# Odd attention: turning the weights on two 64-row halves, with their copies shared anew and four half chunks cast by GpSimd's transfers

## The reference, cut to what matters

```python
H_C, H_C_KV, DH_C = 16, 2, 64       # 16 query heads, 2 key/value heads
s = q @ k.T * 64 ** -0.5 + bias      # banded: own chunk of 64 and the two before
s = where(valid, s, NEG_INF)
p = softmax(concat([s, sink]))[..., :-1]
o = p @ v                            # (S, 16 * 64)
y = o @ w_out                        # 1024 x 1024
```

## Time and profile before

| | |
|---|---|
| median of 3 runs | 1346.29 us (1346.19 to 1346.6) |
| profiled execution | 1346.09 us |
| its span | 1344.2 us |
| TensorE matmuls busy | 1334.3 us, 99% |
| DVE, ACT, GpSimd busy | 974.3, 740.2, 125.3 us |
| granted TensorE clock | 0.999 of full |
| odd attention | about 1079 to 1111 us from the span's start |

### The profile page before, as it was taken

One profiled execution on the slowest core, in us unless ns is written; L12 is line 12 of the kernel. 1 busy time (PEld: TensorE's weight loads), 2 busy tenths in 40 slices (PEclk: granted clock), 3 DMA queues, 4 the chain that ended last, 5 costly groups with the idle time before them and its releaser, 6 DMA issues.

```text
span 1344.2 us, 19217 instructions
## 1 busy us (share of the span) xinstructions
PE 1334.3 (99%) x7365; PEld 1121.7 (83%) x7365; DVE 974.3 (72%) x1502; ACT 740.2 (55%) x1155; POOL 125.3 (9%) x114
## 2 busy tenths in 40 slices
PE   9999999999999999999999999999999999999998
PEld 6888888888888888888888777888888878888886
DVE  7566878777664767877778687886667887786665
ACT  6564555554545754555445676754445675654443
POOL 1000011111000000311111002220000010400000
PEclk9999999999999999999999999999999999999999
DMA  9743545555455334656655524357765524355552
GB/s 375 246 153 129 187 158 193 187 195 192 173 219 186 127 126 160 228 200 231 202 189 201 170 95 151 117 216 227 216 204 193 182 79 173 119 206 193 191 191 88
DMA packets 37673, 244.32 MB, mean 182 GB/s; under 512 B 4656, under 2 KB 5312, under 8 KB 10192
## 3 DMA queue, kind: packets, MB, share of 16 engines
q1 hardware_dynamic: 33568, 228.08, 47.9%
q0 software_dynamic: 3728, 14.82, 3.9%
q10 hardware_dynamic: 288, 0.21, 0.1%
HBM read 241.13 MB, written 1.97 MB: 181 GB/s over the span
## 4 chain that ended last, share of the span: by engine, by line
PE 97%; DVE 1%; ACT 1%; DMA 0%; issue 0%; POOL 0%; ACTq 0%; DVEq 0%
PE ps L1217 19%; PE ps L1155 17%; PE ps L1161 16%; PE ps L1164 16%; PE ps L1224 10%; PE ps L1323 3%; PE ps L1418 2%; PE ps L1449 2%; PE ps L1400 1%; PE ps L2034 1%; PE ps L1265 1%; PE ps L1259 1%; PE ps L1262 1%; PE ps L1577 1%; PE ps L2044 1%; PE ps L1578 1%
## 5 line engine op out<-in xcount | busy, mean ns | idle before, releaser
L2736 DVE TENSOR_TENSOR wlo<-raw,whi 128x1024 fp32r<-128x1024 f32 (+2 forms) x423 | 510.4, 1217 | 264.2 <-ACT whi L2151 263.1
L2151 ACT CAST whi<-raw 128x1024 fp32r<-128x1024 f32 (+1 forms) x431 | 444.6, 1041 | 332.9 <-PE ps L1224 188.5
L1217 PE MATMUL ps<-act,whi 128*128 128x512 f32 x1120 | 266.4, 390 | 0.0
L1217 PEld LDWEIGHTS ps<-act,whi 128*128 128x128 f32 x1120 | 208.4, 188 | 42.2
L1155 PE MATMUL ps<-whi,mhi 128*128 128x512 f32 (+2 forms) x688 | 235.7, 392 | 0.3 <-DVE mlo L2760 0.3
L1161 PE MATMUL ps<-wlo,mhi 128*128 128x512 f32 (+2 forms) x688 | 231.1, 385 | 0.0
L1164 PE MATMUL ps<-whi,mlo 128*128 128x512 f32 (+2 forms) x688 | 231.0, 385 | 0.0
L1164 PEld LDWEIGHTS ps<-whi,mlo 128*128 128x128 f32 x688 | 129.2, 188 | 26.4
L1161 PEld LDWEIGHTS ps<-wlo,mhi 128*128 128x128 f32 x688 | 129.2, 188 | 26.1 <-DVE wlo L2736 0.5
L1224 PEld LDWEIGHTS ps<-act,wlo 128*128 128x128 f32 x1120 | 143.6, 191 | 5.5
L1155 PEld LDWEIGHTS ps<-whi,mhi 128*128 128x128 f32 x688 | 125.9, 188 | 24.1 <-issue 2.4
(11 more groups left out here) (334 smaller groups left out, 1516.3 us busy)
## 6 DMA issues: line engine op xcount, KB each, us to landing
raw<-in_weights SPq DMA_DIRECT2D x210, 1024.0 KB, 4.8
gain_b<-in_norm_g POOLq DMA_DIRECT2D x6, 512.0 KB, 4.0
raw<-in_weights SPq DMA_DIRECT2D x5, 512.0 KB, 5.8
region<-in_b_gate POOLq DMA_DIRECT2D x2, 1024.0 KB, 8.6
o_nat<-in_mem_turned POOLq DMA_DIRECT2D x2, 1024.0 KB, 7.2
region<-band POOLq DMA_DIRECT2D x8, 256.0 KB, 5.0
region<-band POOLq DMA_DIRECT2D x8, 192.0 KB, 5.9
x<-in_x SPq DMA_DIRECT2D x1, 1024.0 KB, 11.6
```

What stands on the lines that cost most here:

```text
L1217: nc.tensor.matmul(ps[:, bank0 + f, :], of(whi, h)[:, k, f * P:f * P + P], act2[:, kx].rearrange("p i n -> p (i n)"), start=kx == 0, stop= ...
L2151: nc.scalar.copy(whi[:, m % HL, 0:w], raw[:, n % RAW, h * w:h * w + w]).then_inc(hi_done, 1)
L2736: nc.vector.tensor_tensor(wlo[:, m % HL, 0:w], raw[:, n % RAW, h * w:h * w + w], whi[:, m % HL, 0:w].bitcast(F32), ALU.subtract).then_inc( ...
```

## The change

`turn` for the odd attention now turns each 128 x 128 block by two transposes of 64 rows, with the identity's matching 64 x 64 part. The halves f = 0 and 1 go to banks 4 and 5. A group takes 384 columns of both banks. `at_x` rises by four behind the group's last transpose, in place of one for each unit. Before a group's first unit TensorE also waits for the copy of the second pair of the group before. The copies read both banks in strips of 64 columns and write the same layout as before. Groups 0, 8, 16 and 24 are now copied by DVE (both pairs), groups 4, 12, 20 and 28 by ACT (both pairs, between its second and third exponential).

The high parts of the four half chunks of `od_w_out`'s first job (0 to 3) are no longer cast by ACT. GpSimd issues a transfer for each, from the weights in HBM straight to the fp32r place in `whi`, as soon as TensorE is done with the half chunk four before it. The issues stand before its first `spread_weights`. ACT skips them; whoever waited for ACT's count waits for the transfer's own semaphore, and DVE's low part waits for the raw chunk too. Every other `wait_ge(hi_done, ...)` becomes `wait_hi`, with the count less the skipped ones.

```diff
--- before.py
+++ after.py
@@ -616,8 +618,10 @@
                     eng = "act" if d["joint"] or d["qt"] else "dve"
+                elif d["deep"]:
+                    eng = ("dve", "dve", "dve", "act")[i // 2 % 4]
                 else:
-                    eng = (("dve", "dve", "dve", "act") if d["deep"] else ("act", "dve", "dve", "dve"))[i // 2 % 4]
+                    eng = ("dve", "act")[i // 4 % 2]
                 n_copies[eng] += d["wide"] or i % (4 if d["joint"] else 2) == 0
@@ -625,6 +629,15 @@
                              [2 * plan.jobs["wo", l][0] + 1 for l in range(DEPTH)] + [2 * plan.jobs["w1", l, 0][0] for l in range(DEPTH)])
+
+        hi_by_dma = [2 * plan.jobs["out2", 1, 0][0] + h for h in range(4)]
+
+        def wait_hi(eng, m):
+
+            if m in hi_by_dma:
+                eng.wait_ge(hi_loaded[hi_by_dma.index(m)], 16)
+            else:
+                eng.wait_ge(hi_done, m + 1 - sum(k < m for k in hi_by_dma))
 
@@ -777,6 +790,16 @@
 
+        def turned_at(u, d):
+
+            return P * (u // 2 % 2), d["w"] // 2
+
+        def turned_by_rows(u, d, b, f):
+
+            first, w = turned_at(u, d)
+            at = first + w * (u % 2) + HD * b
+            return ps[:, 4 + f, at:at + HD]
+
         def pair_width(d):
@@ -785,6 +808,9 @@
                 return ps[:, 4 + d["pair"] % 2, 0:pair_width(d)]
+            if d["halved"]:
+                first, w = turned_at(u, d)
+                return ps[:, 4:6, first:first + 2 * w].rearrange("p f (b j) -> p f b j", j=HD)
             return ps[:, 4 + u // 2 % 2, 0:pair_width(d)]
@@ -798,6 +824,8 @@
                 at = 3072 + 768 * (d["pair"] % 2) + SEQ * d["qt"]
+            if pair and d["halved"]:
+                return work[:, at:at + pair_width(d)].rearrange("p (b f j) -> p f b j", f=2, j=HD)
             if pair:
@@ -1067,6 +1095,12 @@
                                               rden[:, :, HG * g:HG * g + HG].unsqueeze(3).to_broadcast([P, TT, HG, HD])).then_inc(shares_spread, 1)
+
+                    for i, m in enumerate(hi_by_dma):
+
+                        pool.wait_ge(pe_out, 2 * (m - HL + 1))
+                        weights, h = plan.chunks[m // 2][2], m % 2
+                        pool.dma_start(whi[:, m % HL, :], weights[:, h * HALF:h * HALF + HALF]).then_inc(hi_loaded[i], 16)
 
@@ -1413,6 +1447,17 @@
                         wait_copied(pe, u - back)
+                    if d["halved"]:
+
+                        if i % 4 == 0:
+                            wait_copied(pe, u - 2)
+                        for b in range(d["w"] // P):
+                            for f in range(2):
+                                rows_ = slice(HD * f, HD * f + HD)
+                                mm = nc.tensor.transpose(turned_by_rows(u, d, b, f), step_of(1536, u, d)[rows_, b * P:b * P + P], ident[rows_, rows_])
+                        if i % 4 == 3:
+                            mm.then_inc(at_x, 4)
+                        return
                     for b in range(d["w"] // P):
@@ -2133,6 +2178,9 @@
                     m = n_split[0]
+                    if m in hi_by_dma:
+                        n_split[0] += 1
+                        continue
                     n, h = divmod(m, 2)
@@ -2219,12 +2267,12 @@
                             exponents(i + 1)
-                        j = i - 4
-                        if j >= 0 and copied_by[u0 + j][0] == "act":
-                            act.wait_ge(at_x, u0 + j + 2)
-
-                            act.wait_ge(at_o, u0 + j - 4)
-                            nc.scalar.copy(values_of(u0 + j, us[j], True), turned_pair(u0 + j, us[j])).then_inc(at_ya, 1)
+                        for j in (i - 4, i - 2):
+                            if j >= 0 and copied_by[u0 + j][0] == "act":
+                                act.wait_ge(at_x, u0 + j + 2)
+
+                                act.wait_ge(at_o, u0 + j - 4)
+                                nc.scalar.copy(values_of(u0 + j, us[j], True), turned_pair(u0 + j, us[j])).then_inc(at_ya, 1)
                         each(i, True)
@@ -2728,7 +2776,9 @@
                     w = kc // 2 * cols
-                    dve.wait_ge(hi_done, m + 1)
+                    wait_hi(dve, m)
+                    if m in hi_by_dma:
+                        dve.wait_ge(landed[n % RAW], plan.landed[n])
                     if m == 0:
...
                         n_split[0] += 1

```

More of the change, by code:

```diff
@@ L385, in build_network @@
         hi_done = sem("hi_done")
+        hi_loaded = [sem(f"hi_loaded{i}") for i in range(4)]
         lo_done = sem("lo_done")
@@ L605, in build_network @@
                 d["columns"] = k[0] in ("odd", "cross")
+                d["halved"] = k[0] == "odd"
                 d["across"] = d["columns"] or k[0] == "even" and not d["joint"]
@@ L904, in _ @@
                 if n >= RAW:
-                    sp.wait_ge(hi_done, 2 * (n - RAW + 1))
+                    wait_hi(sp, 2 * (n - RAW) + 1)
                     wait_lo(sp, 2 * (n - RAW) + 1)
@@ L945, in split_low @@
                 w = kc // 2 * cols
-                pool.wait_ge(hi_done, m + 1)
+                wait_hi(pool, m)
                 if m >= HL:
@@ L1124, in half_chunk @@
                     stream["need"](place)
-                pe.wait_ge(hi_done, m + 1)
+                wait_hi(pe, m)
                 wh = whi[:, m % HL, 0:kh * cols].rearrange("p (k n) -> p k n", k=kh)
@@ L1212, in turned_chunk @@
                 for h in range(2):
-                    pe.wait_ge(hi_done, 2 * n + h + 1)
+                    wait_hi(pe, 2 * n + h)
                     for f in range(2):
```

## The result

| | before | after |
|---|---|---|
| median (range) of 7 runs each, us | 1346.34 (1346.19 to 1346.62) | 1349.43 (1348.63 to 1352.64) |
| profiled execution, us | 1346.09 | 1349.43 |
| its span, us | 1344.2 | 1347.5 |

Ratio 1.0028 (95% interval 1.0018 to 1.0038): slower by 3 us, beyond the noise, where 0.4 us, a change within it, was forecast, and 0.1 us above the range, which ended at 1349.3. Three of the seven runs of after, at 1351.1 to 1352.6, also show a mean granted clock of 0.997 to 0.998 instead of 0.999 to 1.0; the profiled one is a run without that.

What follows compares the result with a forecast made beforehand. TensorE bounds the kernel now; after the change ACT's loop binds, 2.77 us on average, and with the landing's late start group 28 ends 0.4 us later: profiled 1346.5, median 1346.7, range 1344.8 to 1349.3.

Steps and rivals of the forecast that it cites:

- Theory A: From the experiments: half chunk 0's landing, ahead of DVE's first biased scores, opens a gap of TensorE.
- V24: Measuring point from the experiments: start of the values of group 24, at 1105.80 in the kernel before.
- The rival: Theory A's rival in the experiments: the turns with their signal and copies cost the time.
- the landing: Half chunk 0's transfer, ahead of DVE's first low part: taken as 4.8 us, bounds 3.7 and 8.
- The cover: TensorE's half chunk of weights until 1083.1, plus 0.3, hides late biased scores; next half chunk 0.1 late.
- rival 2: At DVE's low part of half chunk 0, a landing beyond 4.8 decides; over 2.7 us from about 7.5; chance 0.11.
- The turns: TensorE's half-row turns, 0.06 a pair: 0.29 us less a step, 2.3 in eight.
- the form that goes: TensorE's change between scores and turns, 0.15 us, goes in eight steps; net two changes less, 0.3 us.
- Signal and copies: ACT's exponentials wait for the whole group's turns; its copies add 0.75 us in alternate loops; TensorE waits.
- One plain loop: ACT's loop without copies, from one last unit's turn to the next: 2.39 us; with copies 3.14.
- The end: Group 28's last turn, with the heads' cast adding 0.52: at 1106.0 against 1105.6, all behind in TensorE's order.
- The casts that ACT lost: Four ACT casts of 1.05 us in the stage become GpSimd transfers; their removal gives nothing.

Runs made afterwards that it cites:

- all four with the low parts elsewhere: The changed kernel with DVE's low parts moved one place later, behind biased scores that don't need them: 1346.80 us, ratio 1.0006.
- the transfers alone: The kernel before plus the four GpSimd transfers, with full-height turns and the old signal and copy shares: 1349.67 us against 1346.24, ratio 1.0023.
- the turns alone: The changed kernel with ACT casting all half chunks again, keeping half-row turns, group signal and new copy shares: 1346.87 us, ratio 1.0005.
- the signal by unit: The turns alone, but the turns' count rises by one behind each unit; copies still wait for the whole group: 1346.42 us, ratio 1.0002.
- the swapped kernel: The signal by unit with copy shares swapped, ACT copying groups 0, 8, 16, 24 and DVE the others: 1345.90 us, ratio 0.9998.
- the kernel with all copies on DVE: The signal by unit, with DVE making all copies of the odd attention: 1348.44 us, ratio 1.0013.

## Why the prediction was wrong

Theory A is shown, from both sides: the first transfer alone makes the kernel as slow as the whole change does, and all four with the low parts elsewhere make none of that loss. Within the stage, from group 0's scores to V24, the transfers alone cost 1.8 us and the turns alone 0.5, together 2.3 of after's 3.0. The landing was 0.8 longer in after's traced execution than in that of the transfers alone, which fits the other 0.7. The rival holds for the 0.5.

1. **The step that failed: the landing, "I take 4.8".** It took 6.8 us, within the bounds given (3.7 to 8). The issue came at 1076.6 instead of 1076.2 (0.2 of it TensorE's own offset), and the landing took 2.0 longer. So the first four biased scores were over at 1085.93, not 1083.6, 2.3 late. The working compared an average DMA share of 0.81 with idle engines and added 0.8. What the traces show in its place is not a share but an order: 1 MB of SP's was issued 0.3 us ahead, and none of the transfer's packets was moved for at least 3.6 us, against 1.2 into dry engines.
2. **The cover, 0.3 us, was overrun.** The forecast had TensorE 0.1 late at the next half chunk; it was 2.6 late: 2.2 at group 4's scores (the wait of 1.94 and the offset) and 0.4 within the block, where the second wait is 0.32. This is rival 2, given 0.11, in its place and by its mechanism. By its own terms a landing of 6.8 makes 1346.7 + 2.0 - 0.3 = 1348.4, 1.0 short: the issue 0.4 later, and loops that are longer than summed (point 4). Along the forecast's own chain, the last unit of group 8 was turned at 1094.12 instead of 1092.0, 2.1 late, and the rest of the stage added 0.7. So the loss passed 2.7 us at a landing of 6.8 and not of 7.5.
3. **The turns: right.** A pair takes 0.06 where nothing is waited for; behind a wait the second pair of a unit follows after 0.11 (0.06 had been summed). From the last scores to the values the step takes 0.69 instead of 1.11, so 0.42 less; 0.29 for the pairs and 0.15 for the form that goes had been forecast. The rule that a load of 128 columns takes 107 ns (the Trainium skill, TensorE: Matmul & The Clock Gate, LDWEIGHTS) would have them 0.11 apart, and these transposes' rows speak against it, as the earlier trace rows did.
4. **Signal and copies tie TensorE to ACT: right, but the loops were summed too short.** Turns alone gave +0.6 (forecast +0.4), with TensorE's waits of 0.15 for ACT before the last unit in the copying loops. That the two agree is in part luck: the +0.4 has a late start from the landing in it, which the turns alone don't have (group 8 at 1091.48, forecast 1092.0), and their loops are longer. The loop: last turn at 1097.51, exponential at 1097.95 (0.44, as forecast: 0.38, and 0.06 for the second pair), copies 0.73 (0.75). But from group 8 to group 24 the forecast has 11.0 us, and after took 11.7:

```profile
1094.12 0.34 PE L1457 MATMUL ps<-cst,work 64*128 64x64 f32 x4 [0.15 <-ACT work L2262]
1094.60 0.66 PE L1357 MATMUL ps<-cst,proj 128*128 128x128 f32 x4
1095.19 0.88 PE L1494 MATMUL ps<-work,proj 128*64 128x128 f32 x12
...
1105.81 0.34 PE L1457 MATMUL ps<-cst,work 64*128 64x64 f32 x4 [0.15 <-ACT work L2262]
```

"One plain loop", 2.39, failed for group 12: between it and group 8 stand four full turns, the values and the scores, and its turns at 1096.75 wait for nothing, so TensorE's own order bound there, with some 2.9. TensorE's saving of 2.6 us did not arrive; the signal by unit gives back 0.45 of the median and 0.9 of V24.

5. **The end: right in time, with a wait that was not forecast.** Group 28's turns wait 0.76 for DVE's copies of group 24, which stand behind its biased scores. The copies were costed as DVE's load, not as a thing that TensorE waits for. In after the wait cost next to nothing, since ACT was as late: its last exponential of group 28 was over at 1108.63, and V24 followed 0.38 later, as it does 0.32 behind ACT's last in the swapped kernel (1105.12, 1105.44), which has no wait for DVE there. From group 24's last unit to V24 it is 3.2 us, as summed. Only with a signal for each unit, where ACT is done at 1104.63 and V24 comes at 1105.55, does the wait hold TensorE.
6. **The casts that ACT lost gave nothing, and transfers 1 to 3 cost nothing: right**, by the kernel with those alone.

Still open: the runs of the kernels with the first transfer spread up to 3.2 us above their traced executions: after's reach 1352.64, and with half chunk 0 alone the median is 1350.37 against 1348.54. Four of that kernel's five runs above 1350 show a mean granted clock of 0.998, which suggests a clock that fell behind the gap, as it is shown to do behind the longer gap of the kernel with all copies on DVE, for 1.6 us. The fifth, 1350.37, shows 1.0, and there is no trace of such a run with the first transfer. The forecast had no term for it.

## What to carry to other kernels

Before a cast is turned into a transfer, look at who waits for it in its own order: a consumer that stands ahead of critical work on another engine makes the landing the price, and moving that consumer behind the work removed it here and cost nothing that shows. Take a transfer's landing not from idle rows plus a share, but from what other queues have in flight at its issue: nearly all of a 1 MB chunk went ahead of it here. Where a wait for a whole group replaces one for each unit, expect the shorter operation to be given back to the engine that waits: 0.9 us here for the signal alone. And a gap of TensorE can cost more than its length: behind the 2.25 us of one kernel its clock stood at half for 3 us.

## What the runs showed of the hardware

- A transfer from fp32 in HBM to fp32r in SBUF of 512 KB, with no raw chunk in flight (the one at 1083.6 to 1083.8), landed in 3.9, 4.0, 4.0 and 4.5 us in four kernels, like a plain one (4.0). Issued 0.3 us behind a raw chunk of 1 MB of SP's it took 6.8, 6.2, 6.2, 6.1 and 6.0 in five kernels, with or without other transfers of GpSimd's behind it.
- The Trainium skill (DMA: Bandwidth & Descriptors, Anatomy of one DMA) fits a GpSimd transfer with 2.0 us plus bytes at 436 GB/s, 3.2 us here by that estimate. The least that a transfer of this size took is 3.7, a plain one in before on idle engines, so the trace does not agree and the measurement decides.
- Fp32 transposes of 64 rows run side by side on the two halves of the array: twelve matmuls, as six pairs 0.06 apart, in 0.48 us with no step between the scores and them (0.21 to 0.22, one score's streaming).
- Behind a wait of TensorE of 2.25 us (busy 0.38 of the 2 us from 1104 to 1106) the granted clock was 0.50 from 1107 to 1110; behind the waits of 1.94 and 1.34 at group 4's scores the traced executions kept 1.00.
